# ScalarE requests the stores of the gates' tiles itself, with four changes of order beside it

## What is computed

```python
u = rms_norm(h, g_mix[i])
z = u @ w_in[i]
q_a, k_a, v_a, q_b, k_b, v_b, f_b, gate_logits = jnp.split(z, SPLIT_POINTS, axis=-1)
y_a = sliding_window_attention(q_a, k_a, v_a, swa_sinks[i]) @ w_br_swa[i]
y_b = forgetting_attention(q_b, k_b, v_b, f_b + b_forget[i]) @ w_br_fox[i]
gates = jax.nn.sigmoid(gate_logits).reshape(B, S, N_BRANCH, D_MODEL)
mixed = gates[:, :, 0] * y_a + gates[:, :, 1] * y_b
h = h + mixed @ w_mix_out[i]
h = h + jnp.square(jax.nn.relu(rms_norm(h, g_mlp[i]) @ w_ff1[i])) @ w_ff2[i]
ple_gate = jax.nn.sigmoid(rms_norm(h, g_ple[i]) @ w_ple_gate[i])
h = h + ple_gate * (p[i] @ w_ple_proj[i])
```

## Time and profile before

| | |
|---|---|
| median of 3 runs | 1704.05 us (1703.57 to 1704.71) |
| the profiled execution, its own time | 1705.43 us |
| its span, first to last instruction | 1703.6 us |
| TensorE busy | 1690.8 us, 99% of the span |
| VectorE busy | 1210.8 us, 71% |
| ScalarE busy | 751.2 us, 44% |
| GpSimd busy | 241.7 us, 14% |

### The profile page before, as it was taken

How to read it: one execution, slowest core, us unless ns; L and a number is a source line. 1 busy time by engine, 2 the same in 40 slices (tenths; PEclk the granted TensorE clock), 3 DMA queues, 4 the chain that set the end, 5 groups by cost and what they waited for, 6 DMA issues and landing times.

```text
span 1703.6 us, 20481 instructions
## 1 busy us (share of the span) xinstructions
PE 1690.8 (99%) x8111; PEld 1418.5 (83%) x8111; DVE 1210.8 (71%) x1463; ACT 751.2 (44%) x1116; POOL 241.7 (14%) x226
## 2 busy tenths in 40 slices
PE   9999999999999999999999999999999999999998
PEld 7888887888999888888888888888888888888886
DVE  5573457553798785388974985698498747999788
ACT  7233366663698431253323332332334427535434
POOL 1000011110487225100000000000000234100002
PEclk9999999999999999999999999999999999999999
DMA  9286996779772776066247216432821224885322
GB/s 335 86 322 249 341 347 220 248 270 307 180 152 55 235 245 249 1 226 231 99 159 282 78 59 257 153 99 99 296 74 38 87 68 158 319 326 210 118 99 99
DMA packets 146735, 318.38 MB, mean 187 GB/s; under 512 B 10000, under 2 KB 21840, under 8 KB 141264
## 3 DMA queue, kind: packets, MB, share of 16 engines
q1 hardware_dynamic: 146208, 316.49, 54.1%
q10 hardware_dynamic: 432, 0.59, 0.1%
HBM read 231.03 MB, written 86.02 MB: 186 GB/s over the span
## 4 chain that ended last, share of the span: by engine, by line
PE 89%; DVE 5%; ACT 2%; issue 1%; DMA 1%; POOL 1%; SPq 0%; POOLq 0%; DVEq 0%; ACTq 0%
PE PS L1131 11%; PE PS L1133 11%; PE PS L1132 11%; PE PS L847 9%; PE PS L848 9%; PE PS L849 9%; PE PS L822 4%; PE PS L1202 3%; PE PS L1203 3%; PE PS L1204 3%; PE PS L1023 2%; PE PS L1025 2%; PE PS L1024 2%; PE PS L1045 2%; PE PS L1066 1%
## 5 line engine op out<-in xcount | busy, mean ns | idle before, releaser
L1235 ACT ACTIVATE WH<-WB 128x2048 fp32r<-128x2048 f32 x56 | 107.3, 1917 | 285.0 <-PE PS L1133 238.0
L1774 DVE TENSOR_TENSOR WB<-WB,WH 128x2048 fp32r<-128x2048 f32 x56 | 128.2, 2288 | 96.5 <-ACT WH L1235 96.5
L1131 PE MATMUL PS<-WH,AH 128*128 128x512 f32 x448 | 174.8, 390 | 0.7 <-DVE UF L2141 0.7
L1131 PE MATMUL PS<-AH,WH 128*128 128x512 f32 x448 | 174.6, 390 | 0.0
L1133 PE MATMUL PS<-WH,AL 128*128 128x512 f32 x448 | 174.3, 389 | 0.0
L1133 PE MATMUL PS<-AH,WB 128*128 128x512 f32 x448 | 174.3, 389 | 0.0
L1132 PE MATMUL PS<-WB,AH 128*128 128x512 f32 x448 | 174.3, 389 | 0.0
L1132 PE MATMUL PS<-AL,WH 128*128 128x512 f32 x448 | 174.3, 389 | 0.0
L2733 POOL TENSOR_SCALAR SM<-SM 128x1 f32<-128x1 f32 x47 | 33.3, 708 | 857.8 <-ACT SQ L1246 632.2
L847 PE MATMUL PS<-RHL,UH 128*128 128x512 f32 x320 | 125.8, 393 | 0.0
L849 PE MATMUL PS<-RHL,UL 128*128 128x512 f32 x320 | 124.7, 390 | 0.0
(11 more groups left out here) (337 smaller groups left out, 4148.9 us busy)
## 6 DMA issues: line engine op xcount, KB each, us to landing
WB<-in_w_ff SPq DMA_DIRECT2D x32, 1024.0 KB, 9.3
AH<-uf_scratch SPq DMA_DIRECT2D x21, 1024.0 KB, 5.4
AL<-uf_scratch SPq DMA_DIRECT2D x21, 1024.0 KB, 7.5
GX<-gates_scratch SPq DMA_DIRECT2D x64, 256.0 KB, 3.7
gates_scratch<-GST SPq DMA_DIRECT2D x56, 256.0 KB, 3.9
H<-in_x SPq DMA_DIRECT2D x16, 512.0 KB, 9.5
RAW<-in_w_in SPq DMA_DIRECT2D x16, 512.0 KB, 8.0
UH<-ugT_scratch SPq DMA_DIRECT2D x8, 1024.0 KB, 7.2
```

What stands on the lines that cost most here:

```text
L1131: pe.matmul(bank(b), sh[:, q], mh, start=(k == 0 and kind.fresh), stop=False, skip_group_check=True)
L1235: return act.activation(dst, src, ACT.Copy, **more)
L1774: return dve.tensor_tensor(dst, src, high.bitcast(F32), ALU.subtract)
```

## The change

ScalarE requests the 56 stores of the gates' tiles; each waits for ScalarE's own copy to be done (SP still waits for the copies, as its pace, but requests none of the stores). Beside it: (1) at the start ScalarE requests the first half of the weight ahead of the identity, and there is a third idle product; (2) the block sum S2 of the second half stands behind the window's work of its place, not ahead of it; (3) the block sum S4 and the low part behind it stand one place later (step 6, place 2 and not 1); (4) `tok_low(8)` stands behind the last sum of step 6, not ahead of it.

```diff
@@ tensor
             on.wait_ge(*zeros_set.of())
-            idle_products(2)
+            idle_products(3)
             on.wait_ge(*ident_in.of())
             p_to_columns(0, 0)
             idle_products(1)
@@ scalar, start
-            act.dma_start(ident, A["c_mats"][0]).then_inc(*ident_in.up())
             for k in range(2):
                 act.dma_start(p_weight(PWR[:, 4:8, :], 0)[:, k, :], w_pp[P * k:P * k + P, 0:512]).then_inc(*pw_in[0, k].up())
+                if k == 0:
+                    act.dma_start(ident, A["c_mats"][0]).then_inc(*ident_in.up())
@@ scalar, gates and windows
                     on.wait_ge(*(gate_out[s].of(n - 1, s) if n else t_out.all()))
                     copy(GST[s][:, :], bank(s)).then_inc(*gate_copied.up(n, s))
+                    on.wait_ge(*gate_copied.of(n, s))
+                    u, p = g_order[n]
+                    act.dma_start(gates_d[u, p - 1, s, :, :], GST[s][:, :]).then_inc(*gate_out[s].up(n, s))
@@ vector, gates and windows
                     if n == 4 and k in (5, 7):
                         gate_wide_sum(1, "S1" if k == 5 else "S3")
-                    if n == 5 and k == 5:
-                        gate_wide_sum(1, "S2")
                     if n == 13 and k in (3, 5):
                         split_to(S_vb.idx[k // 4])
                     for v in swa_steps[8 * n + k]:
                         window(*v)
-                    if (n, k) == (6, 1):
+                    if (n, k) == (5, 5):
+                        gate_wide_sum(1, "S2")
+                    if (n, k) == (6, 2):
                         gate_wide_sum(1, "S4")
                         gate_low(7, 0)
@@ vector, MLP
             hidden_sum(1, "S1")
             sum_of(6, 2)
-            tok_low(8)
             for n in range(7, 54):
                 u, i = n // 7, n % 7
                 sum_of(n - 1, 3)
+                if n == 7:
+                    tok_low(8)
@@ sync, gates and windows
                     on.wait_ge(*gate_copied.of(n, s))
-                    sp.dma_start(gates_d[u, p - 1, s, :, :], GST[s][:, :]).then_inc(*gate_out[s].up(n, s))
```

## The result

| | before | after |
|---|---|---|
| median | 1704.28 us (1703.52 to 1705.43, 20 runs) | 1706.11 us (1703.91 to 1712.17, 20 runs) |
| ratio | | 1.0015, 95% interval 1.0009 to 1.0021 |
| the profiled execution | 1705.43 us, span 1703.6 | 1710.46 us, span 1708.6 |

The change costs 1.8 us by the medians; 1703.4 was forecast, 0.7 us less than before. The times of after also spread: five of the 20 lie between 1709.9 and 1712.2, all others at or under 1707.0, and no run of before is over 1705.43. The ratio stands for more than the 1.8 us: 0.0015 is 2.6 us, which is the difference of the means (1706.94 and 1704.33), and half of that comes from the five. The profiled execution is one of the five. A second profile of the same kernel, from the middle of its times, is in the experiments.

What follows compares the result with a forecast made beforehand. TensorE, busy 1690.8 of 1703.6 us, was taken to bound the kernel. Terms +2.0 +0.5 -2.7 -0.7 +0.3 give -0.6 us: 1704.8 from the profiled 1705.43, and 1703.4 for the median, 1.4 lower; range 1700.2 to 1706.6.

Steps and rivals of the forecast that it cites:

- The sum: Whole kernel: all terms added give -0.6 us against the profiled execution; chance 0.5.
- The stores' own chain: Copies to `GST` from 236 to 273 us: five stores on ScalarE make TensorE lose 2.0 us.
- `tok_low(8)`: MLP near 817 us: adding the awaited tile ahead of the low part gains 0.7 us.
- TensorE waits for none of them but `QS`: SP's loads, asked for some 0.3 us earlier without the store requests: worth nothing to TensorE.
- all four stalls go: TensorE at 280 to 300 us: moving S2 and S4 removes four stalls, the last on `QS`; -2.7 us.
- +0.3 for the start: Start: the identity lands later, first product at about 7.6 instead of 7.0 us; +0.3 us, bounds -1.4 and +0.9.
- The price of a store: Each store's wait and request on ScalarE costs it 0.44 to 0.55 us, taken as 0.5.
- Rival 1: Stores on ScalarE: a request is nearly free, 0.1 us or less; 1701.7 us, chance 0.14.
- Nobody on TensorE's path waits for a store: Stores leaving the queue they share with 1 MB loads: worth nothing.
- rival 3: Start: the clock rises early, 1.4 us less instead of 0.3 more; 1701.7 us, chance 0.12.
- Behind 300 us: Stores after 300 us: slack mostly 1 to 5 us, one tight place at 330 us; +0.5 us.
- Rival 2: Stores on ScalarE: requests coinciding with SP's make each store cost 1.0 us; slower, 1706.4 us, chance 0.14.

Runs made afterwards that it cites:

- e9: The changed kernel run again with no edit, for a second profile; median 1705.82 us, ratio 1.0006 to the kernel before.
- e7: Kernel before with S2 and S4 moved and ScalarE requesting each store one tile later, not waiting for its own last copy; 1702.30 us, ratio 0.9988.
- e1: The changed kernel with the stores requested by SP, as before, and all changes of order kept; 1703.37 us, ratio 0.9991 to the kernel before.
- e3: Kernel before with only S2 and S4 moved; 1702.64 us, ratio 0.9990.
- e8: Kernel before with only S2, S4 and `tok_low(8)` moved; 1701.57 us, ratio 0.9984.
- e2: Kernel before with only the stores moved to ScalarE, no change of order; 1709.47 us, ratio 1.0029.
- e4: Kernel before with the stores moved to ScalarE and S2 and S4 moved; 1705.75 us, ratio 1.0008.
- e12: The changed kernel, but SP requests the nine stores from the last of step 5 to the last of step 7; 1706.26 us, ratio 1.0010 to before.
- e6: Kernel before with S2 and S4 moved and GpSimd waiting for the copies and requesting the stores; 1706.86 us, ratio 1.0012.
- e11: Kernel before with S2 and S4 moved, stores with SP, ScalarE waiting for each of its copies but requesting nothing; 1702.19 us, ratio 0.9988.
- e14: Kernel before with S2, S4 and `tok_low(8)` moved, stores with SP, four added 256 KB transfers at step 6 on SP's queue; 1703.31 us, ratio 0.9992.
- e15: Kernel before with S2, S4 and `tok_low(8)` moved and ScalarE requesting each store one tile later, without waiting for its own copy; 1701.76 us, ratio 0.9987.
- e13: Kernel before with S2, S4 and `tok_low(8)` moved, stores with SP, four added 256 KB transfers at step 6 on ScalarE's queue; 1702.51 us, ratio 0.9989.
- e10: The changed kernel with each store requested one tile later, behind the next tile's copy; 1702.70 us, ratio 0.9991 to the kernel before.

## Why the prediction was wrong, point by point

**Which steps failed.** The sum was -0.6 us; the medians say +1.8 and the means +2.6. The stores' own chain and `tok_low(8)` came out as summed. What failed is what the sum says of SP's loads and of the start: "TensorE waits for none of them but `QS`. That is worth nothing" (`UL` cost 1.1 us in e9, the largest single miss), "`QS` is there at 298 to 299.3. So all four stalls go" (it was there at 299.9 in e9 and at 303.65, 3.5 us later than before, in the long execution that was profiled; the fourth stall stayed), and +0.3 for the start (it was +0.6 and +1.1 in the two profiles).

**The price of a store: right in size, wrong in its reason.** 0.44 to 0.55 us was forecast and 0.5 taken; the rows have 0.50 to 0.56. The chain to 273 us lost 2.1 us against the 2.0 predicted. But I added request and wait as two separate costs. They are one: the request (0.33) is free unless the wait (0.13) has emptied the engine first. Rival 1, the free request, is true of a store that does not wait for its own copy (e7).

**QS: a step that failed.** "Comes to the scores at about 299.4 of the old clock, and `QS` is there at 298 to 299.3. So all four stalls go: -2.7." The three stalls on `OA` and `PRL` went (1.7 us in my sum, 2.2 by TensorE's starts, since each had a slow restart behind it), and S4 now follows window 7's bias as foreseen:

```profile
285.79 0.41 DVE L1986 CUSTOM_DVE_ANT_0 T<-PS,BIAS 128x256 f32<-128x256 f32 x1
...
287.59 2.29 DVE L1942 TENSOR_TENSOR GR<-Gd,Gc 128x2048 f32<-128x2048 f32 x1
289.91 2.36 DVE L1778 TENSOR_TENSOR GR<-GR,GR 128x1024 fp32r<-128x1024 f32 x2
```

The fourth did not. I wrote that the DMA engines are busy with `UH` and `UL` ahead, and then moved TensorE by the 2.0 us of the stores but left the request of `UL` where it was. SP waits for the same copies: `UL`, and `QS` behind it, move by the 2 us too. Redone with the rows I had: 298 to 299.3 for the sums alone, 2.0 later with the stores, makes 300.0 to 301.3 against TensorE at 299.4, a wait of 0.6 to 1.9. Measured: 0.7 us (e9) and 2.9 us. On the old clock (e9 is 2.2 us behind before at 236 us, by start and `UL`) e9 has TensorE at the scores at 299.3, as predicted, and `QS` at 299.9. Even without the stores 0.6 to 1.5 us remain (e1, e3, e8), since the removed stalls bring TensorE forward as well. The stall at the scores, 1.1 us with its restart before, is 1.2 in e3 and 0.9 in e9, so the whole term was worth -2.1 and -2.4, not -2.7; in the first profile the same stretch lost 2.3, with the wait for `UL` (0.9) and the slow clock in it.

**The clock, no step at all.** I priced a stall at its length. One of 2.9 us brought the granted clock down to half for 3.4 us, 1.7 us more; one of 0.7 us (e9) did not:

```profile
302.00:305.00 3.00, 2.75 (x14) 2.42 (x15) 2.93 (x13) 0.94 (x3) 0.00 (x0) 1.00 1.05 401
```

**SP's queue.** "TensorE waits for none of them but `QS`" fell with the two waits for `UL` (0.7 at 295 us in the first profile, 0.8 at 221 in e9). With the slow restart the one of e9 costs TensorE 1.1 us. Waits like it, at 219 to 221 us, are in the profiles of e2 (1.4), e4 (0.6) and e12 (0.5), which all have the stores on ScalarE behind their own copies, and not in those of before, e1, e3, e6, e7, e8, e11, e14 and e15, nor in the first profile of after. But one of 1.1 us is also in e13, with the stores at SP and nothing changed before it, so such waits come without the change too. What speaks for the change is e10: it differs from the changed kernel only in that no store waits for its own copy, and is 3.1 us faster by the medians (1702.7 against 1705.8 in e9), of which the chain is 2.1. About 1 us of waits for `UL` seems to hang on it; in what way is not shown. "Nobody on TensorE's path waits for a store. Nothing again" missed the long runs: five of 20 at 3.8 to 6.1 us above the median, which alone raise the mean by 1.3 us.

**`tok_low(8)`: right.** Predicted -0.7, TensorE's starts give -0.8 (after, e8, e9). VectorE adds the tile ahead of the low part, and TensorE waits at line 1131 no more; the small stall passed to step 8, as said:

```profile
820.22 0.68 DVE L2145 TENSOR_TENSOR UF<-UF,PS 128x512 f32<-128x512 f32 x1
...
821.54 2.28 DVE L1778 TENSOR_TENSOR AL<-UF,AH 128x2048 fp32r<-128x2048 f32 x1
```

**The start: right sign, too small.** Predicted +0.3, bounds -1.4 and +0.9. After, against the earlier trace rows:

```profile
1.20 4.49 DMA CST<-in_c_mats
...
5.74 1.12 PE PS L822 x4
...
8.56 0.43 PE PS L899
```

The identity landed at 5.7 us, not at 4.9 to 5.2, and by the timeline the first product started at 8.2 us, not at 7.6. The step that was mis-sized is that of the landing: "when the first 320 KB have" took over a time from another order of requests. What held it up by another half us (SP's loads are asked for at the same time) I did not test. TensorE lost 0.6 us here in the first profile and 1.1 in e9.

These two are no measure of the change alone, for the start differs from execution to execution. In the twelve profiles with the old start TensorE is at 12 us between 1.4 us ahead of before and 0.8 behind it, mostly by the clock: steps of 0.23 us begin ahead of 8.5 us in eight of them and at 9.8 to 11.5 in four, before among these. With the new start they begin at 10.4 to 11.2 in four of five, and ahead of 8.5 only in e10, which is 1.2 us ahead of before at 12 us. So the early clock, my rival 3, is what most executions of the old start have, and few of the new. In the new start TensorE stands for the identity, 1.1 to 1.6 us, just before its transposes; but it does in e10 too (1.5), and that this is why the clock rises later is not shown. By the mean of the profiles the new start costs 1.1 us, and by the runs that differ in it alone 1.2 us (ratio 0.9991 in e1, 0.9984 in e8) and 0.7 (0.9991 in e10, 0.9987 in e15); the intervals overlap.

**Behind 300 us: right.** Predicted +0.5, measured +0.4 and +0.2 at 380 to 400 us.

Added up for e9, the common case: stores +2.1 and +0.2, S2 and S4 with `QS` -2.4, `tok_low(8)` -0.8, start +1.1, `UL` +1.1, together +1.3; its execution is 1.2 us above the one profiled before. `UL` (1.1), the start (0.8) and `QS` (0.3) went against me, and the long runs come on top. That the medians of 1705.8 and 1706.1 lie within the stated 1700.2 to 1706.6 is the width of the range; its sign was wrong. (The upper end is 0.2 us beyond rival 2, not the half us that I wrote.) Rival 2, slower at 1706.4 us, had the right number for a wrong reason: in this stage no request took ScalarE longer than 0.40 us, beside one of SP or not.

## What to carry to other kernels

A DMA request is nearly free on a computing engine as long as it does not wait for that engine's own last instruction: put it one tile later, or leave it on an engine that has nothing else to do then, as SP was here; GpSimd, idle too, was no such place (e6). When a chain becomes later, move every request that keeps pace with it, too, before comparing arrivals; a request asked for earlier into a full DMA lands earlier by less than that (6.45 us against 3.3 in e3). Price a stall of some us on TensorE with the slow clock behind it, and look at the spread of the times, not at the median alone. One profile of each side does not measure a change of 1 us at the start: before one reads it, the same start has to be looked at in other runs.

## What the hardware did that I had not expected

- A request of 64 bytes kept ScalarE's queue 0.23 us, one of 256 KB 0.33, and neither kept its engine when it did not wait.
- A stand of 2.9 us (after) and of 2.7 us (e6) were each followed by 3.4 us at a granted clock of 0.5; stands of 0.6 to 1.5 us by none.
- The same 1 MB took 5.7 us to land in one execution of the changed kernel and 9.7 in another, where fifteen of its sixteen parts had come after 6.2.
- The clock at the start rose between 7.7 and 11.2 us in executions of kernels with the same start (e10, e9), and between 7.5 and 11.5 with the old one (e11, e13).
